# Expert rows added into one array of sums by accumulating scatters, and the last two experts' rows finished on their own

## The chip, the cores and the metric

The kernel runs on one core of a Trainium2 chip. The metric is the device time of one execution in microseconds; the profiled span runs from the first to the last instruction of one execution. Every data transfer runs on the core's 16 DMA engines, whichever queue issues it.

## The reference, cut to what matters

One encoder layer is computed for two inputs with the same parameters: 256 tokens of a prompt and 1024 of a sample, each of width D = 1024, in float32. After a mixer and a residual (`x1` below) comes a mixture of experts, and then the final norm:

```python
e = group * 8 + top2                      # two experts of one group for each token
y[t] = sum over its two experts of w * down(silu(x @ gate) * (x @ up))
out = rmsnorm(x1 + y, final_norm_g)
```

There are 32 experts in 4 groups of 8; a token picks one group and two experts inside it. The 1280 tokens of both inputs give 2560 expert rows of 1024 floats (4 KB each), and every token needs both of its rows before it can be normalised.

## The kernel before, in words

The kernel is written engine by engine, with semaphores set by hand. T = 1280 tokens are NT = 10 tiles of P = 128. The stages are: projection, mixer, output projection with the router (tile by tile), the experts, and a tail.

**The experts.** Step i treats expert i of an order that takes the four groups in turn (`expert_at`), so four experts in a row share no token. n_half is read at run time; here it is 16, so there are 32 steps (steps 0 to 3 are written out, the others stand in a loop of two steps per turn). A list in DRAM holds, for every expert, the rows of its tokens; positions beyond the list's length hold an index out of bounds, which an indirect transfer leaves out. In each step

- SP loads 12 pieces of 512 KB of weights (`piece_in`, L680) into a ring of NST = 12 slots `e_st`. A piece is loaded when the slot's last user is split.
- ACT rounds a piece to `e_hi` (`hi_part`, L1533) and DVE subtracts to get `e_lo` (`lo_part`, L2037), in rings of NRG = 6. PE multiplies (`product3`, L937 to L939): 8 gate and up pieces of expert i, then 4 down pieces of expert i-1.
- POOL gathers the token rows of a later expert (`rows_in`, L850), their weights (`weights_in`, L871), and scatters the output rows of expert i-2 (`rows_out`, L858 to L861) from `yo` to `y_dram` ("expert_rows"), once ACT and DVE have copied them from PSUM (`y_half`, L1600 and L2119). There are two buffers `yo`, and each `y_half` waits for the scatter before it on the same buffer.

`y_dram` has 2T rows: a token's first expert writes row t, its second row T + t. Which of the two is first is decided in the routing (`route_rest`, L2000 to L2005, with `swapped`, `entry` and `turn_sizes`), such that the first rows are all written early.

**The tail.** All of `x1` stays in SBUF. After the loop POOL adds the first rows of tiles 0 to 4 onto `x1` by five direct accumulating transfers (`add_rows`, L877), SP loads those of tiles 5 to 9 to free slots of `e_st` (L736), and, once the scatters of the last two experts have landed, SP loads the second rows of all ten tiles (L743). DVE adds (L2188, L2195), or PE does by products with the identity (`first_row_part` L1291, `second_row_part` L1299); ACT takes the sum of squares and the root (L1656, L1657), DVE scales (`final_norm`, L2199 and L2203), SP stores (L746).

The wait that separates the early part of the tail from its late part is SP's:

```python
            for b in range(2):
                sp.wait_ge(y_out[b], 16 * n_half)
            for t in LATE_ORDER:
                slot = late_slot(t)
                if slot < NT - N_ADDED:
                    sp.wait_ge(f_sum, slot + 1)
                sp.dma_start(spare(slot), y_dram[T + t * P:T + (t + 1) * P, :]).then_inc(e_load[slot], 16)
```

Each queue works in program order. POOL's DMAs, direct and indirect, share one queue of descriptors, SP's another.

Of the kernel before, what the change touches and what calls it, by code (L numbers as in the profile page):

```python
# [15 lines left out]
P = 128  # L16
# [5 lines left out]
def build(nc, x_prompt, x_sample, norm1_g, w_in, pool_w, pool_scale, gate_b, head_norm_g, w_out,  # L22
# [27 lines left out]
    y_dram = nc.dram_tensor("expert_rows", (2 * T, D), F32).ap()  # L50
# [49 lines left out]
    entry = const("entry", [P, NT, 2], I32)  # L100
    swapped = const("swapped", [P, NT])
    turn_sizes = const("turn_sizes", [P, 2])
# [119 lines left out]
    rows_to = mbuf("rows_to", [P, NT * E + 1], I32)  # L222
    row_of = mbuf("row_of", [P, 2], I32)
    row_to = mbuf("row_to", [P, 2], I32)
# [3 lines left out]
    w_row = at("w_row", ROWS + KB, [P, 2], F32)  # L228

    gf_b = at("gf_b", ROWS + 4 * KB, [P, D], F32)  # L230
    N_ADDED = 5

    def spare(slot):

        return e_st[:, slot, :, :].rearrange("p a n -> p (a n)")

    def early_slot(t):

        return t - N_ADDED

    def late_slot(t):

        return (5 + t) % NST

    LAST_ROUTED, LAST_OUT = 2, 0
    SQUARES = 3
    ON_PE = (2, 4, 5, 7, 8, 9)
    LATE_ORDER = (0, 2, 1, 3, 4, 5, 6, 7, 8, 9)
# [10 lines left out]
    with ctx:  # L259
# [3 lines left out]
        def sem(name):  # L263
# [28 lines left out]
        rows_added = [sem(f"rows_added{i}") for i in range(NT // 2)]  # L292
# [21 lines left out]
        gx_load = [sem(f"gx_load{i}") for i in range(2)]  # L314
        ehi_done, elo_done, piece_used, no_row, gx_zero, ext_ready, exhi_done, exlo_done = (
# [7 lines left out]
        f_out, f_sum, f_pe_sum, f_root, f_done = (  # L323
            sem(n) for n in ("f_out", "f_sum", "f_pe_sum", "f_root", "f_done"))
# [153 lines left out]

        def late_loads(t, last):

            return 16 * (last + (3 if late_slot(t) < NT - N_ADDED else 2))

        def sums_taken(t):

            return NT - N_ADDED + sum(x not in ON_PE for x in range(t + 1))

        def pe_sum(t):

            return two((0, 2, 6, 4)[ON_PE.index(t) % 4])

# [22 lines left out]
        def _(sp):  # L513
# [230 lines left out]
            for t in range(NT):  # L744
                sp.wait_ge(f_done, t + 1)
                sp.dma_start(tokens(t, y_prompt, y_sample), x1[:, t, :]).then_inc(f_out, 16)  # L746
            sp.wait_ge(f_out, 16 * NT)


        @block.gpsimd  # L750
        def _(pool):
# [46 lines left out]
            for part, size in enumerate((float(T), -float(T))):  # L798
                pool.memset(turn_sizes[:, part:part + 1], size).then_inc(pool_step, 1)
            pool.wait_ge(pool_step, 21)  # L800
# [18 lines left out]
            def entries_out(i):  # L819
                pool.wait_ge(slots_done, 2 * i + 2)  # L820
                for k in range(2):
                    pool.indirect_dma_start(
                        out=list_dram, out_offset=bass.IndirectOffsetOnAxis(ap=slot_i[:, i, k:k + 1], axis=0),
                        in_=entry[:, order[i], k:k + 1], in_offset=None).then_inc(list_out[i % 2], 16)

            for i, t in enumerate(order):
                pool.wait_ge(xn2_done, i + 1)
# [26 lines left out]

            def rows_out(i, b):
                pool.wait_ge(y_left, i + 1)
                pool.wait_ge(y_right, i + 1)
                pool.tensor_copy(row_to[:, b:b + 1], rows_to[:, bass.ds(i, 1)]).then_inc(row_placed, 1)  # L858
                pool.wait_ge(row_placed, i + 1)
                pool.sem_inc(pool_past, 1)  # L860
                pool.indirect_dma_start(  # L861
                    out=y_dram, out_offset=bass.IndirectOffsetOnAxis(ap=row_to[:, b:b + 1], axis=0),
                    in_=yo[:, b, :], in_offset=None, bounds_check=2 * T - 1, oob_is_err=False).then_inc(y_out[b], 16)

            def weights_in(i, b):

                if isinstance(i, int):
                    rows = rows_to[:, i:i + 1] if i else first_row[:, :]
                else:
                    rows = row_of[:, b:b + 1]  # L870
# [4 lines left out]

            def add_rows(t):
                pool.dma_start(x1[:, t, :], y_dram[t * P:(t + 1) * P, :], accum_op=ALU.add).then_inc(rows_added[t], 16)  # L877
# [16 lines left out]
            rows_in(3, 1)  # L894
            rows_out(0, 0)
# [13 lines left out]
            for b in range(2):  # L909
                pool.wait_ge(y_out[b], 16 * n_half - 32)  # L910
                pool.sem_inc(pool_past, 1)
            for t in range(N_ADDED):
                add_rows(t)
            for b in range(2):
                pool.wait_ge(y_out[b], 16 * n_half - 16)
                pool.sem_inc(pool_past, 1)
            for b in range(2):
                pool.tensor_copy(row_to[:, b:b + 1],
# [1320 lines left out]
```

## Time and profile before

| | |
|---|---|
| median of 3 runs | 1171.67 us (1170.9 to 1173.81) |
| profiled execution, its own time | 1169.87 us |
| its span | 1168.1 us |
| busy share of PE, DVE, ACT, POOL | 98%, 73%, 60%, 23% |
| DMA moved | 324.11 MB, mean 277 GB/s |
| packets of the two queues in use, share of 16 engines | SP 65.1%, POOL 10.5% |

A busy share is an average over all stages. The time of the profiled execution is 1.8 us above its span (start and end of the program lie outside), and 1.8 us below the median of the runs. Of the DMA queues, "hardware_dynamic" (q1) is SP's here and "software_dynamic" (q0) is POOL's; a share of 100% means that 16 engines were occupied all the time.

### The profile page before, as it was taken

What the parts mean: (1) busy time and instruction counts of PE and PEld (TensorE: products, weight loads), DVE (VectorE), ACT (ScalarE), POOL (GpSimd) and SP (SyncE); (2) the same over time, 40 slices, a digit from 0 to 9 for tenths busy, and PEclk for the clock granted to TensorE, in tenths of its full rate; (3) what the DMA queues carried; (4) which work ended last, traced back from release to release, by engine and by line L of the source; (5) the groups of instructions that cost most, each with busy time, mean ns of one, the idle gap of its engine ahead of it and who ended that gap; (6) DMA issues with size and microseconds to landing.
All of it is one profiled execution on the core that took longest, in us unless ns stands there. A gap on an engine that the chain in (4) does not pass through costs nothing.

```text
span 1168.1 us, 18708 instructions
## 1 busy us (share of the span) xinstructions
PE 1142.5 (98%) x5934; PEld 962.9 (82%) x5934; DVE 857.4 (73%) x1340; ACT 699.1 (60%) x1134; POOL 273.3 (23%) x348
## 2 busy tenths in 40 slices
PE   8999999999999999999999999999999999999987
PEld 8988888888889888887888888888888888888863
DVE  6649510134437766677899999999999999999957
ACT  6342241233438744334788787787887887887834
POOL 2200210001200012223142332332332325443320
PEclk9999999999999999999999999999999999999999
DMA  7312240446969644444999999999999999999989
GB/s 223 90 36 83 90 136 1 128 144 220 312 242 365 219 139 157 155 176 157 390 407 388 396 386 401 381 399 386 388 385 393 387 386 392 379 398 388 381 253 359
DMA packets 137795, 324.11 MB, mean 277 GB/s; under 512 B 25526, under 2 KB 62304, under 8 KB 137744
## 3 DMA queue, kind: packets, MB, share of 16 engines
q1 hardware_dynamic: 120032, 279.18, 65.1%
q0 software_dynamic: 17712, 44.27, 10.5%
q8 instruction: 30, 0.49, 0.2%
q14 instruction: 21, 0.17, 0.0%
HBM read 285.37 MB, written 51.12 MB: 288 GB/s over the span
## 4 chain that ended last, share of the span: by engine, by line
PE 63%; DMA 25%; DVE 6%; issue 3%; ACT 2%; SPq 0%; ACTq 0%; DVEq 0%; POOLq 0%
DMA e_st<-in_expert_w_down_dram 19%; PE psum L937 17%; PE psum L939 17%; PE psum L938 17%; DVE e_lo L2037 3%; DMA units<-mlstm_units 1%; PE psum L1127 1%; ACT e_hi L1533 1%; DMA e_st<-in_expert_w_gate_dram 1%; PE psum L1221 1%; PE psum L951 1%; PE psum L1062 1%; DMA e_st<-in_expert_w_up_dram 1%; PE psum L1063 1%; PE psum L1299 1%
## 5 line engine op out<-in xcount | busy, mean ns | idle before, releaser
L2037 DVE TENSOR_TENSOR e_lo<-e_st,e_hi 128x1024 fp32r<-128x1024 f32 x384 | 447.0, 1217 | 26.4 <-ACT e_hi L1533 25.6
L1533 ACT ACTIVATE e_hi<-e_st 128x1024 fp32r<-128x1024 f32 x384 | 388.3, 1056 | 50.8 <-DMA e_st<-in_expert_w_down_dram 35.1
L939 PE MATMUL psum<-e_hi,ex_lo 128*128 128x512 f32 x512 | 199.5, 390 | 0.0
L937 PE MATMUL psum<-e_hi,ex_hi 128*128 128x512 f32 x512 | 199.4, 389 | 0.0
L938 PE MATMUL psum<-e_lo,ex_hi 128*128 128x512 f32 x512 | 199.2, 389 | 0.0
L937 PE MATMUL psum<-xT_hi,w_hi 128*128 128x512 f32 (+1 forms) x432 | 151.1, 350 | 2.2 <-DVE w_lo L1673 1.4
L939 PE MATMUL psum<-xT_hi,w_lo 128*128 128x512 f32 (+1 forms) x432 | 149.4, 346 | 0.0
L938 PE MATMUL psum<-xT_lo,w_hi 128*128 128x512 f32 (+1 forms) x432 | 149.2, 345 | 0.0
L858 POOL COPY row_to<-rows_to 128x1 int32 (+1 forms) x30 | 46.6, 1554 | 295.2 <-DVE yo L2119 295.2
L937 PEld LDWEIGHTS psum<-e_hi,ex_hi 128*128 128x128 f32 x512 | 96.1, 188 | 20.2 <-DVE ex_lo L2108 0.2
L939 PEld LDWEIGHTS psum<-e_hi,ex_lo 128*128 128x128 f32 x512 | 96.1, 188 | 20.0
L938 PEld LDWEIGHTS psum<-e_lo,ex_hi 128*128 128x128 f32 x512 | 96.1, 188 | 19.9
L937 PE MATMUL psum<-e_hi,ht_hi 128*128 128x512 f32 x256 | 105.8, 413 | 3.5 <-DVE e_lo L2037 2.4
L939 PE MATMUL psum<-e_hi,ht_lo 128*128 128x512 f32 x256 | 100.9, 394 | 0.0
L938 PE MATMUL psum<-e_lo,ht_hi 128*128 128x512 f32 x256 | 100.6, 393 | 0.0
L937 PEld LDWEIGHTS psum<-xT_hi,w_hi 128*128 128x128 f32 x432 | 82.3, 191 | 12.3 <-DVE w_lo L1673 1.6
L1673 DVE TENSOR_TENSOR w_lo<-w_st,w_hi 128x1024 fp32r<-128x1024 f32 x21 | 25.6, 1222 | 90.0 <-ACT w_hi L1329 90.0
L939 PEld LDWEIGHTS psum<-xT_hi,w_lo 128*128 128x128 f32 x432 | 82.1, 190 | 9.9
L938 PEld LDWEIGHTS psum<-xT_lo,w_hi 128*128 128x128 f32 x432 | 82.3, 191 | 9.7
L937 PE MATMUL psum<-wo_hi,mix_hi 128*128 128x512 f32 x160 | 64.5, 403 | 0.0
L939 PE MATMUL psum<-wo_hi,mix_lo 128*128 128x512 f32 x160 | 62.6, 391 | 0.0
L938 PE MATMUL psum<-wo_lo,mix_hi 128*128 128x512 f32 x160 | 62.3, 389 | 0.0
(292 smaller groups left out, 1857.2 us busy)
## 6 DMA issues: line engine op xcount, KB each, us to landing
e_st<-in_expert_w_gate_dram SPq DMA_DIRECT2D x128, 512.0 KB, 13.6
e_st<-in_expert_w_up_dram SPq DMA_DIRECT2D x128, 512.0 KB, 13.7
e_st<-in_expert_w_down_dram SPq DMA_DIRECT2D x128, 512.0 KB, 14.5
mlstm_units<-stage SPq DMA_DIRECT2D x18, 640.0 KB, 3.9
w_st<-in_w_in_dram SPq DMA_DIRECT2D x20, 512.0 KB, 4.4
xn_scratch<-xn POOLq DMA_DIRECT2D x20, 512.0 KB, 3.9
stage<-gate_rows SPq DMA_DIRECT2D x18, 512.0 KB, 5.8
e_st<-expert_rows SPq DMA_DIRECT2D x15, 512.0 KB, 10.0
```

Source lines behind the costliest of these rows:

```text
L858: pool.tensor_copy(row_to[:, b:b + 1], rows_to[:, bass.ds(i, 1)]).then_inc(row_placed, 1)
L937: pe.matmul(out, a_hi, b_hi, start=start, stop=False)
L938: pe.matmul(out, a_hi, b_lo, start=False, stop=False)
L939: return pe.matmul(out, a_lo, b_hi, start=False, stop=stop)
L951: last = pe.transpose(psum[:, 4 + 2 * (t % 2) + k // 4, (k % 4) * P:(k % 4 + 1) * P], xn[:, t % 2, k:D:KD], ident[:, :])
L1062: pe.matmul(out, unit_part(n, H + h), state[:, d, h, :], start=True, stop=False)
L1063: last = pe.matmul(out, unit_part(n, h), v[:, ck, h, :], start=from_zero(step), stop=True)
L1127: last = pe.matmul(psum[:, 7, 0:NL], x1T[:, k, :], rw[:, k, :], start=(k == 0), stop=(k == KD - 1))
L1221: last = pe.transpose(psum[:, 2 + half, (k % 4) * P:(k % 4 + 1) * P], gx[:, b, k:D:KD], ident[:, :])
L1533: act.activation(e_hi[:, r, :, :], e_st[:, slot, :, :], ACT.Copy).then_inc(ehi_done, 1)
L1673: dve.tensor_tensor(w_lo[:, m % 4, :, :], w_st[:, m % 2, :, :], w_hi[:, m % 4, :, :].bitcast(F32), ALU.subtract).then_inc(wlo_done, 1)
L2037: dve.tensor_tensor(e_lo[:, r, :, :], e_st[:, slot, :, :], e_hi[:, r, :, :].bitcast(F32), ALU.subtract).then_inc(elo_done, 1)
```

## The change

One array `sum_dram` ("row_sums") of T rows takes the place of `y_dram` with 2T.

- In the output-projection stage POOL stores each tile of `x1` to `sum_dram`, ahead of the two stores of `xn2`.
- `rows_out` scatters with an addition (`compute_op=ALU.add`) at the token's row. The indices `tokens_to` are made from the lists by two POOL operations before the first scatter.
- The decision on which expert comes first (`swapped`, `entry`, `turn_sizes`) is gone, with two DVE operations per tile and three after the last tile.
- In the tail, SP waits until all scatters but those of the last two experts have landed and loads all ten tiles of sums over `x1`. Tiles are normalised and stored as they come. POOL gathers the sums of the last two experts' tokens to `gx`; DVE adds the rows from PSUM (`late_total`), and the finished rows go by four indirect scatters to the two outputs, after every tile's store has landed, since the tiles have stale values in those rows.
- The last expert's products go to other PSUM banks (`bank=0`), so PE doesn't wait for `y_half`; PE takes no part in the tail's sums. The filler products `keep_busy` alternate between two banks.

```diff
@@ SP, tail
             sp.wait_ge(elo_done, down_piece(last, 3)[0] + 1)
             for b in range(2):
-                sp.wait_ge(y_out[b], 16 * n_half - 32)
-            for t in range(N_ADDED, NT):
-                slot = early_slot(t)
-                sp.dma_start(spare(slot), y_dram[t * P:(t + 1) * P, :]).then_inc(e_load[slot], 16)
-            for b in range(2):
-                sp.wait_ge(y_out[b], 16 * n_half)
-            for t in LATE_ORDER:
-                slot = late_slot(t)
-                if slot < NT - N_ADDED:
-                    sp.wait_ge(f_sum, slot + 1)
-                sp.dma_start(spare(slot), y_dram[T + t * P:T + (t + 1) * P, :]).then_inc(e_load[slot], 16)
-            for t in range(NT):
-                sp.wait_ge(f_done, t + 1)
-                sp.dma_start(tokens(t, y_prompt, y_sample), x1[:, t, :]).then_inc(f_out, 16)
+                sp.wait_ge(y_out[b], 16 * n_half - 16)
+            for t in (0, 1, 2, 3, 8, 9, 4, 5, 6, 7):
+                sp.dma_start(x1[:, t, :], sum_dram[t * P:(t + 1) * P, :]).then_inc(e_load[t] if t < 8 else sum_load[t - 8], 16)
+            for t in TAIL:
+                if t in range(NT):
+                    sp.wait_ge(f_done, TAIL_AT[t] + 1)
+                    sp.dma_start(tokens(t, y_prompt, y_sample), x1[:, t, :]).then_inc(f_out, 16)
             sp.wait_ge(f_out, 16 * NT)
+            sp.wait_ge(late_out, 16 * 4)
@@ POOL
             for i, t in enumerate(order):
+                pool.wait_ge(x1_done, i + 1 if i < NT - 1 else NT + 1)
+                pool.dma_start(sum_dram[t * P:(t + 1) * P, :], x1[:, t, :]).then_inc(sums_out, 16)
                 pool.wait_ge(xn2_done, i + 1)
...
             def rows_out(i, b):
                 pool.wait_ge(y_left, i + 1)
                 pool.wait_ge(y_right, i + 1)
-                pool.tensor_copy(row_to[:, b:b + 1], rows_to[:, bass.ds(i, 1)]).then_inc(row_placed, 1)
-                pool.wait_ge(row_placed, i + 1)
-                pool.sem_inc(pool_past, 1)
+                token_rows(i, b)
                 pool.indirect_dma_start(
-                    out=y_dram, out_offset=bass.IndirectOffsetOnAxis(ap=row_to[:, b:b + 1], axis=0),
-                    in_=yo[:, b, :], in_offset=None, bounds_check=2 * T - 1, oob_is_err=False).then_inc(y_out[b], 16)
+                    out=sum_dram, out_offset=bass.IndirectOffsetOnAxis(ap=token_of[:, b:b + 1], axis=0),
+                    in_=yo[:, b, :], in_offset=None, bounds_check=T - 1, oob_is_err=False,
+                    compute_op=ALU.add).then_inc(y_out[b], 16)
...
-            for t in range(N_ADDED):
-                add_rows(t)
...
+            pool.wait_ge(ext_ready, 4 * n_half + 2)
+            pool.sem_inc(pool_past, 1)
             for b in range(2):
                 pool.indirect_dma_start(
-                    out=y_dram, out_offset=bass.IndirectOffsetOnAxis(ap=row_to[:, b:b + 1], axis=0),
-                    in_=yo[:, b, :], in_offset=None, bounds_check=2 * T - 1, oob_is_err=False).then_inc(y_out[b], 16)
+                    out=gx[:, b, :], out_offset=None, in_=sum_dram,
+                    in_offset=bass.IndirectOffsetOnAxis(ap=token_of[:, b:b + 1], axis=0),
+                    bounds_check=T - 1, oob_is_err=False).then_inc(late_load[b], 16)
...
+            pool.wait_ge(f_out, 16 * NT)
+            for b in range(2):
+                pool.wait_ge(f_done, TAIL_AT[f"late {b}"] + 1)
+                pool.indirect_dma_start(
+                    out=y_sample[0, :, :], out_offset=bass.IndirectOffsetOnAxis(ap=late_to[:, b:b + 1], axis=0),
+                    in_=yo[:, b, :], in_offset=None, bounds_check=S1 - 1, oob_is_err=False).then_inc(late_out, 16)
+                pool.indirect_dma_start(
+                    out=y_prompt[0, :, :], out_offset=bass.IndirectOffsetOnAxis(ap=token_of[:, b:b + 1], axis=0),
+                    in_=yo[:, b, :], in_offset=None, bounds_check=S0 - 1, oob_is_err=False).then_inc(late_out, 16)
@@ ACT, tail (root(x) waits for the tile's load, or for late_sum, then squares and root as before)
-            y_half(last_i - 1, 0, down_piece(last_i, 3)[0] + 1)
-            for c in range(1, 4):
-                hi_part(last_piece(last_i, c))
-            y_half(last_i, 1, last_piece(last_i, 3)[0] + 1)
+            hi_part(last_piece(last_i, 1))
+            hi_part(last_piece(last_i, 2))
             act.activation(wts[:, 3, 0:1], epsc[:, :], ACT.Sqrt)
+            hi_part(last_piece(last_i, 3))
+            for x in TAIL:
+                root(x)
@@ DVE, tail (TAIL = [0, 1, 2, 3, "late 0", 8, 9, 4, "late 1", 5, 6, 7])
+            lo_part(last_piece(last_i, 1))
+            lo_part(last_piece(last_i, 2))
+            final_norm(0)
+            lo_part(last_piece(last_i, 3))
+            for x in TAIL[1:]:
+                if x == 2:
+                    late_total(0)
+                if x == 9:
+                    late_total(1)
+                final_norm(x)
```

On POOL, the end of the program before, from the loop's last scatter on (`expert_rows` is `y_dram`; L877 are the direct accumulating transfers, L927 the scatters of the last two experts):

```order
L861 DMA expert_rows<-yo,row_to 2560x1024
L871 DMA w_row<-entry_weights,row_of 128x1
L902 ISA
L902 COMPARE_AND_BRANCH
L910 ISA
L877 DMA x_136<-expert_rows 128x1024 x5
L915 REGISTER_ALU
L918 ISA
L918 COPY row_to<-rows_to 128x1
L918 ISA
L918 COPY row_to<-rows_to 128x1
L927 DMA expert_rows<-yo,row_to 2560x1024 x2
```

and the same place now, behind the loop (`row_sums` is `sum_dram`; L893 gathers sums, L905 and L908 write to the outputs):

```order
L886 COPY token_of<-tokens_to 128x1
L886 ISA
L886 COPY token_of<-tokens_to 128x1
L890 ISA
L893 DMA gx<-row_sums,token_of 128x1024 x2
L897 TENSOR_SCALAR late_far<-token_of 128x2
L898 TENSOR_SCALAR late_to<-token_of 128x2
L900 TENSOR_TENSOR late_to<-late_to,late_far 128x2
L905 DMA out_dram<-yo,late_to 1024x1024
L908 DMA out_dram<-yo,token_of 256x1024
L905 DMA out_dram<-yo,late_to 1024x1024
L908 DMA out_dram<-yo,token_of 256x1024
```

The direct additions are gone (the scatters in the loop add), and four scatters to the outputs close the queue, the first of them behind the wait for all stores.

On DVE, the tail before, from the last weight piece's split (L2037) on:

```order
L2037 TENSOR_TENSOR e_lo<-e_st,e_hi 128x1024
L465 ISA
L2119 COPY yo<-psum 128x512
L2187 ISA
L2188 TENSOR_TENSOR x_136<-x_136,e_st 128x1024 x5
L2195 TENSOR_TENSOR x_136<-x_136,e_st 128x1024 x2
L2199 RECIPROCAL wts<-wts 128x1
L2203 SCALAR_TENSOR_TENSOR x_136<-x_136,wts,gf_b 128x1024
```

and now, from the split of the last piece but one (L1982 is `lo_part`, L2125 `late_total`, L2136 and L2139 `final_norm`):

```order
L1982 TENSOR_TENSOR e_lo<-e_st,e_hi 128x1024
L2136 RECIPROCAL wts<-wts 128x1
L2139 SCALAR_TENSOR_TENSOR x_133<-x_133,wts,gf_b 128x1024
L1981 REGISTER_ALU
L1982 TENSOR_TENSOR e_lo<-e_st,e_hi 128x1024
L2136 RECIPROCAL wts<-wts 128x1
L2139 SCALAR_TENSOR_TENSOR x_133<-x_133,wts,gf_b 128x1024
L2123 REGISTER_ALU
L2125 TENSOR_TENSOR yo<-gx,psum 128x1024
```

The split of the last weight piece stands behind the first tile's scaling, and nine additions have become two.

## Rows read from the trace of the kernel before

**Rows 1.** Windows: us, each engine's busy time, TensorE's clock, DMA share, GB/s.
```profile
600.00:700.00 100.00, 100.00 (x471) 83.67 (x470) 94.91 (x96) 81.48 (x98) 31.91 (x30) 1.00 1.01 392
1000.00:1100.00 100.00, 99.60 (x472) 82.87 (x471) 93.75 (x96) 81.79 (x96) 38.50 (x28) 1.00 1.01 388
```

**Rows 2.** Timeline of ACT: the gate's activation in two steps running.
```profile
595.49 0.60 ACT L1605 ACTIVATE sg<-psum 128x512 f32<-128x512 f32 x1 [1.61 <-PE psum L939]
613.26 0.60 ACT L1605 ACTIVATE sg<-psum 128x512 f32<-128x512 f32 x1 [1.61 <-PE psum L939]
```

**Rows 3.** ACT's wait and the weight loads' landings (L680), 600 to 700 us.
```profile
ACT e_hi L1533 <- DMA e_st<-in_expert_w_down_dram: 0.2, 1, 0.2
DMA to landing us min/median/max: 10.9/13.0/14.1
```

**Rows 4.** The same (us in total, times, longest), 1000 to 1100 us.
```profile
ACT e_hi L1533 <- DMA e_st<-in_expert_w_down_dram: 10.0, 17, 1.5
DMA to landing us min/median/max: 11.5/14.7/16.4
```

**Rows 5.** DMA queues, 600 to 1100 us: packets, MB, share of 16 engines.
```profile
q1 hardware_dynamic: 48480, 176.54, 91.5%
q0 software_dynamic: 9075, 18.42, 9.6%
```

**Rows 6.** DMA queues, 1117 to 1124 us, with the direct accumulating transfers.
```profile
q0 software_dynamic: 256, 0.93, 66.9%
q1 hardware_dynamic: 255, 0.95, 36.7%
```

**Rows 7.** DMA queues, 806 to 809 us, around one plain scatter of the loop.
```profile
q1 hardware_dynamic: 266, 0.98, 80.6%
q0 software_dynamic: 156, 0.24, 21.5%
```

**Rows 8.** Window 1131 to 1138 us (columns as in rows 1), and its DMA queues.
```profile
1131.00:1138.00 7.00, 7.00 (x27) 5.07 (x27) 3.68 (x3) 0.49 (x2) 1.00 (x1) 0.98 0.50 198
...
q1 hardware_dynamic: 209, 0.74, 26.1%
q0 software_dynamic: 232, 0.63, 23.4%
```

**Rows 9.** The chain that ended last: start us, us, what.
```profile
1104.26 20.32 DMA e_st<-in_expert_w_down_dram
...
1130.99 7.20 DMA expert_rows<-yo,row_to
```

**Rows 10.** Timeline of ACT in the tail: one tile's square and root.
```profile
1149.69 1.06 ACT L1656 ACTIVATE e_st<-x 128x1024 f32<-128x1024 f32 x1
...
1150.87 0.29 ACT L1657 ACTIVATE wts<-wts,epsc 128x1 f32<-128x1 f32 x1
```

**Rows 11.** DVE in the tail: two tiles' scalings, and the group of late additions.
```profile
1149.00 0.15 DVE L2199 RECIPROCAL wts<-wts 128x1 f32<-128x1 f32 x1
...
1150.39 0.16 DVE L2199 RECIPROCAL wts<-wts 128x1 f32<-128x1 f32 x1
...
L2195 DVE TENSOR_TENSOR x<-x,e_st 128x1024 f32<-128x1024 f32 x4 | 4.9, 1222 | 3.1 <-DMA e_st<-expert_rows 3.1
```

**Rows 12.** The stores of the outputs (L746): issue to landing.
```profile
DMA to landing us min/median/max: 2.9/5.0/7.8
```

**Rows 13.** The list scatters of 4-byte rows (L822): landing, and two issues running.
```profile
DMA to landing us min/median/max: 2.3/3.4/8.8
...
430.33 1.04 POOL L822 DMA_INDIRECT row_lists<-entry,slot_i  x1 [0.30 <-issue]
431.68 1.01 POOL L822 DMA_INDIRECT row_lists<-entry,slot_i  x1 [0.30 <-issue]
```

**Rows 14.** Window 1128 to 1131 us: TensorE's clock after a wait for weights.
```profile
1128.00:1131.00 3.00, 3.00 (x9) 2.32 (x8) 0.69 (x1) 1.60 (x2) 0.01 (x1) 0.50 1.01 326
```

**Rows 15.** Timeline of DVE in the last tile's routing: an operation that goes.
```profile
542.18 0.22 DVE L2003 SCALAR_TENSOR_TENSOR entry<-turn_sizes,swapped,rowval 128x2 int32<-128x2 f32 x1
```

More of the change, by code:

```diff
@@ L314, in build @@
         gx_load = [sem(f"gx_load{i}") for i in range(2)]
+        late_load = [sem(f"late_load{i}") for i in range(2)]
+        sum_load = [sem(f"sum_load{i}") for i in range(2)]
+        sums_out, late_sum, late_out = sem("sums_out"), sem("late_sum"), sem("late_out")
         ehi_done, elo_done, piece_used, no_row, gx_zero, ext_ready, exhi_done, exlo_done = (
@@ L477, in expert_at @@
             return (i % GR) * EPG + (i // GR) % EPG
[L479 to L489, printed above, removed]
         def load_half_steps(eng):
@@ L1206, in _ @@
             for t in range(NT):
-                last = pe.matmul(psum[:, 5, 0:E], onesb[:, :], chosen[:, t, :], start=(t == 0), stop=(t == NT - 1))
+                last = pe.matmul(psum[:, 6, 0:E], onesb[:, :], chosen[:, t, :], start=(t == 0), stop=(t == NT - 1))
             last.then_inc(totals_ready, 1)
@@ L1235, in gate_up, with down @@
                     last.then_inc(piece_used, 1)
-            def down(piece, i, b, turned=None):
+            def down(piece, i, b, turned=None, bank=4):
                 pe.wait_ge(htlo_done, i + 1)
-                wait(pe, y_left, i)
-                wait(pe, y_right, i)
+                if bank == 4:
+                    wait(pe, y_left, i)
+                    wait(pe, y_right, i)
                 for c in range(4):
@@ L1245, in down @@
                     for half in range(2):
-                        last = product3(psum[:, 4 + half, :], (ht_hi[:, b, c, :], ht_lo[:, b, c, :]),
+                        last = product3(psum[:, bank + half, :], (ht_hi[:, b, c, :], ht_lo[:, b, c, :]),
                                         (e_hi[:, r, half, :], e_lo[:, r, half, :]), c == 0, c == 3)
@@ L1275, in _ @@
             last_i = 2 * n_half - 1
[L1276 to L1312 removed]
+            down(lambda c: last_piece(last_i, c), last_i, 1, bank=0)
         @block.scalar
@@ L2201, in final_norm @@
+            def final_norm(x):
+                dve.wait_ge(f_root, TAIL_AT[x] + 1)
+                if x in range(NT):
+                    rms, out = wts[:, 3, x:x + 1], x1[:, x, :]
+                else:
+                    k = int(x == "late 1")
+                    rms, out = stat[:, 1, k:k + 1], yo[:, k, :]
+                link(dve.reciprocal(rms, rms))
+                if x == TAIL[0]:
                     dve.wait_ge(norms_in, 48)
-                out = x1[:, t, :].rearrange("p (a n) -> p a n", a=2)
@@ L2203, in final_norm @@
-                dve.scalar_tensor_tensor(out=out, in0=pe_sum(t) if t in ON_PE else out, scalar=wts[:, 3, t:t + 1],
-                                         in1=gf_b[:, :].rearrange("p (a n) -> p a n", a=2),
+                dve.scalar_tensor_tensor(out=out, in0=out, scalar=rms, in1=gf_b[:, :],
                                          op0=ALU.mult, op1=ALU.mult).then_inc(f_done, 1)
-            for t in range(N_ADDED, NT):
-                early_sum(t)
-            for t in range(NT + 2):
-                if t < NT and t not in ON_PE:
-                    late_sum(t)
-                if t >= 2:
-                    final_norm(t - 2)
+            lo_part(last_piece(last_i, 1))
```

163 lines of the change are left out of this document (52 added, 111 removed).

## The prediction

> **What bounds the kernel now.** I read the windows first, then the waits and landings of the weight loads, then the DMA queues, and the chain last. In the expert stretch PE is busy without a gap, DVE 94 to 95% and the DMA engines 101% (packets overlap a little), at some 390 GB/s [rows 1]. The step repeats every 17.77 us (613.26 - 595.49), with ACT waiting for PE before the activation [rows 2]: PE sets the pace there. But the DMA engines are no looser. Between 600 and 700 us ACT waits 0.2 us for weights, and a weight load lands 13.0 us after its issue [rows 3]; between 1000 and 1100 us it waits 10.0 us, and the landing takes 14.7 us [rows 4]. Weights thus come later from step to step while PE holds its pace: the DMA engines need slightly more than 17.77 us a step, and by 1000 us the cushion is used up. Work added to them has nowhere to hide. In the tail the chain goes through the last weight load (20.32 us in place of 14.7), the last expert's scatter, 7.20 us [rows 9], the second rows' loads, and DVE's scaling.
>
> **What a plain row and an added row cost an engine.** From 600 to 1100 us SP's queue moves 176.54 MB, 43,100 packets of 4 KB, in 91.5% of 16 x 500 us: 0.17 us each. POOL's moves 18.42 MB, 4,497 rows, over 28 gathers and 28 scatters: 80 rows each [rows 5]. Beside the direct accumulating transfers POOL's queue moves 0.93 MB, 227 rows, in 66.9% of 16 x 7 us: 0.33 us each, while a weight packet beside them keeps 0.18 (0.95 MB in 36.7%) [rows 6]. An addition costs an engine 0.33 - 0.17 = **0.16 us a row** more. These additions go from DRAM to SBUF; none from SBUF to DRAM is in the trace. I take the same price: it is one read of the source and one of the destination through the engine either way. Its bounds are 0 (the second read runs beside the first) and 0.33 (each read waits for the other and the write). [...]
>
> **Which engines pay.** Spread over all 16, 80 rows are 5 to an engine. The trace speaks against that. Where both queues are busy an engine takes a packet of each in turn, so that an even scatter would hold half of all engine time; around a scatter of 59 rows (0.24 MB) POOL's queue holds 21.5% of three microseconds [rows 7], as if it ran on some eight engines for 2.6 us. At 1131 to 1138 us, with the last scatters and some leftover loads, the engines are busy 0.50 of the time, although both queues have work left: about half of the engines work, the others are through [rows 8]. So eight engines carry most of each scatter, 8 to 10 rows, and they are the ones that come late. I take **8 rows on the busiest engine** (the list fills positions from 0, and the last 16 of 80 fall to others). Bounds: 5 and 10.
>
> **The loop.** Thirty scatters become additions (experts 0 to 29): 30 x 8 x 0.16 = **+38.4 us** on the engines that hold up the weights, bounds 0 to 30 x 10 x 0.33 = 99. A step becomes 17.8 + 1.3 = 19.1 us. POOL's own share is nothing: it waits for `yo` in every step, the copy of the indices replaces a copy, and the two operations on 320 indices stand in an idle stretch before the first scatter.
>
> **Before the loop.** Ten stores of x1 (512 KB each) go out in a stage in which the engines are half idle; the last is issued shortly before the stores of xn2 that the first gather waits for, which may cost up to its 8 x 0.16 = 1.3 us. Two DVE operations fewer in the last tile's routing (0.22 us the longer one [rows 15]) and three in the weights give back up to five times that. I take -0.3 in all, from bounds of +1.3 and -1.1.
>
> **The tail, rebuilt.** (1) The last weights were issued at 1104.3 and took 20.32 us because five additions (640 rows of 0.33) and five early loads ran beside them [rows 9]; now only the two gathers of late sums do, 2 x 8 rows x 0.16 = 2.6 us. They land at 1104.3 + 14.7 [rows 4] + 38.4 + 2.6 = 1160.0. (2) The gain vector and the first tile of sums follow in the same queue, 8 packets of 0.16 us an engine each: 1162.6. The waits before those loads (the split of the last step's down pieces, the scatters of experts 28 and 29) are over some 5 us earlier. (3) ACT's square and root, 1.06 to 1151.16 - 1149.69 = 1.5 us [rows 10], for the first tile: 1164.1. (4) DVE then has twelve scalings at 1.39 us (1150.39 - 1149.00), two late totals and the last split at 1.22 [rows 11]: 20.3 us, the last at 1184.4. ACT needs 12 x 1.5 = 18 and the loads and stores 20 x 1.3 = 26 us from 1160.0 on, so DMA keeps up with DVE to within a store or two: the last store lands 3 to 4 us later [rows 12], **1188**. (5) New: POOL then issues four scatters. It starts 0.9 us after its release, the next three follow at 1.35 us (431.68 - 430.33), and the last lands between 2.3 us (4-byte rows [rows 13]) and 7.2 us (behind other work [rows 9]) after its issue. Its rows are 4 KB, with the engines idle: 4 us. 1188 + 0.9 + 4.0 + 4.0 = 1196.9; with -0.3, **1196.6**, against 1168.1: **+28.5 us**.
>
> Without the loop's 38.4 the change would save 9.9 us, for it takes PE's sums and the wait for the last scatter off the end, and puts one round of stores and scatters on it. The sum is against the profiled execution of 1169.87, hence 1198.4; the median lies 1.8 above that execution: **1200 us**.
>
> A rule that speaks for a milder end: around a full stretch the rows show 388 to 392 GB/s [rows 1]. The Trainium skill, "DMA: Bandwidth & Descriptors", Where 436 GB/s comes from, puts the limit for transfers with HBM at about 358 GB/s on the HBM side. By that rule bytes count, not the busiest engine: 0.33 MB more to read a step. The measured rate is above it, so it isn't the limit here; its form of the sum is the first rival.
>
> **The rivals.**
> - *Even load.* If all 16 engines share the added work, or if total bytes decide: 30 x 80 x 0.16 / 16 = 24 us instead of 38.4, so about **1186**. For it: the engines are 101% busy on average. Against it: rows 7 and 8. Chance 0.15.
> - *The second read is free* (faster, the other side). If an addition from SBUF reads its two sources, in two memories, side by side, a row costs 0.17 us as before, the step stays at 17.8, and the tail's 9.9 us are all that is left: **1162**. It decides below 9.9 / 240 = 0.04 us more a row. Against it: 0.33 in rows 6, where the sources also lie in two memories. Chance 0.11.
> - *Dearer additions*, another 0.17 us a row: 240 x 0.17 = 41 us more, **1241**. Chance 0.06.
> - *TensorE's clock.* After waiting for the last weights PE ran at 0.50 of its clock, 1.2 GHz [rows 14]. If the 1.3 us that PE now waits in each step bring that about now and then, steps grow further; at 3 us of half clock a step (1.5 us lost, of which 1.3 were idle anyway) and some restarts, +10: **1210**. Chance 0.06.
> - *Nothing measurable:* the cushions before and in the loop take all and the tail is as long as before, **1171**. A measurement can tell about 0.3% from no change. Chance 0.02.
>
> **How the numbers follow.** My forecast keeps 0.60. The range of 1182 to 1217 takes in the even load and the clock, and 9 or 10 rows on the busiest engine (+5 to +10), and leaves out the free read, the dearer one and no change, 0.19. Faster 0.11, same 0.02, slower 0.87.
>
> **What would show it.** The gate's activations 19.1 us apart late in the loop; POOL's scatter packets at 0.33 us (q0 near 13% of the engines with some 80 rows a transfer); ACT's waits for weights 1 to 2 us a step from the start, and PE waiting for `e_lo`; landings of weight loads near 15.5 us; a last weight landing near 1160; DVE without gaps for 20 us; some 9 us from the last store to the end. Wrong if activations stay 17.8 us apart (the read is free), or are 18.6 apart (even load), or if PE's clock leaves 1.00 in the loop.

## The result, and the profile after

| | before | after |
|---|---|---|
| median (range, runs) | 1172.74 us (1170.9 to 1179.68, 4) | 1198.75 us (1196.06 to 1201.53, 4) |
| profiled span | 1168.1 us | 1195.9 us |
| first and last activation of the gate | 563.8, 1112.1 | 564.7, 1150.2 |
| from the last activation to the end | 56.1 us | 45.7 us |

After against before is 1.0228, with an interval of 1.02 to 1.0257: slower. 1200 us was predicted.

The gate's activation runs once in a step, 32 times. Its group shows first and last start in one row, and so where a difference lies. Below is the group in the trace after (min/median/max in ns, first and last start in us).

```profile
L1551 ACT ACTIVATE sg<-psum x32: 574/581/602, 564.7 to 1150.2; 128x512 f32<-128x512 f32 x32
```

In the trace before it is this row:

```profile
L1605 ACT ACTIVATE sg<-psum x32: 577/597/602, 563.8 to 1112.1; 128x512 f32<-128x512 f32 x32
```

From the first to the last it was 548.2 us and is 585.5 (the timelines have 563.84 to 1112.05 and 564.66 to 1150.19): the 31 steps between them take 37.3 us more, and what follows takes 10.3 less (the start of the experts is 0.8 later). The net is the 27.8 us between the spans. The first of the 31 steps takes some 14 us in both traces; the 30 behind it take 17.8 us each before and 19.0 now.

The windows of the loop in the trace after, columns as in [rows 1]:

```profile
600.00:700.00 100.00, 97.28 (x456) 80.37 (x455) 92.20 (x95) 79.43 (x92) 28.27 (x26) 1.00 1.01 372
1000.00:1100.00 100.00, 95.51 (x446) 78.20 (x445) 88.53 (x89) 78.97 (x90) 27.00 (x25) 1.00 1.01 369
```

PE no longer fills the window, while the DMA engines stay at 101% with fewer bytes: 372 and 369 GB/s in place of 392 and 388 [rows 1]. The same occupation moves less. The DMA queues from 600 to 1100 us show whose packets grew:

```profile
q1 hardware_dynamic: 45359, 165.16, 86.4%
q0 software_dynamic: 8464, 17.50, 13.9%
```

POOL's queue holds 13.9% with 17.50 MB, where it held 9.6% with 18.42 MB [rows 5]. That is 0.26 us for a 4 KB row in place of 0.17, over gathers and scatters together; the gathers are half of them, so a scattered row costs about 0.35. Two of the waits, ACT's for weights and PE's for `hh` from DVE, first from 600 to 700 us (us in total, times, longest):

```profile
ACT e_hi L1479 <- DMA e_st<-in_expert_w_down_dram: 7.4, 10, 2.4
...
PE psum L1237 <- DVE hh L2070: 2.5, 2, 1.5
```

And from 1000 to 1100 us; the last line is the landings of the weight loads (L655) in the same stretch:

```profile
ACT e_hi L1479 <- DMA e_st<-in_expert_w_down_dram: 12.5, 14, 2.7
...
PE psum L1237 <- DVE hh L2070: 4.5, 4, 1.6
...
DMA to landing us min/median/max: 12.2/16.2/17.1
```

From 600 to 700 us ACT already waits 7.4 us for down weights, where it waited 0.2 [rows 3], and from 1000 to 1100 us a load lands after 16.2 us in place of 14.7 [rows 4]. The cushion that lasted up to 1000 us before is gone by 600. What PE waits for is `hh`, which DVE makes behind the splits of the late weights, and hardly ever `e_lo`, which the forecast had named. The chain that ended last says the same from the other side:

```profile
DMA e_st<-in_expert_w_down_dram 30%; PE psum L918 13%; PE psum L920 13%; PE psum L919 13%; DVE e_lo L1982 5%; ACT e_hi L1479 2%; PE psum L1044 2%; PE psum L1108 1%; PE psum L1043 1%; PE psum L1051 1%; SPq L655 1%; PE psum L932 1%; DVE x L2139 1%; PE psum L1089 1%; PE psum L964 1%
```

Thirty per cent of the whole span are landings of down weights, where the chain of the kernel before had 19%. The tail's chain, start and length in us:

```profile
1165.92 1.28 DVE x L2139
...
1179.59 1.30 DVE x L2139
1180.90 2.64 DMA out_dram<-x
...
1184.44 0.38 POOL out_dram L905
...
1185.80 1.00 POOL out_dram L908
...
1188.38 0.97 POOL out_dram L908
```

DVE scales without a gap, the last store lands at 1183.54, and the four scatters are issued between 1184.4 and 1189.35. The span ends at 1195.9, 6.5 us after the last issue is done. In that stretch the trace has one instruction left on POOL's sequencer, DRAIN, at the end of its program. It starts at 1185.9, lasts 9.8 us and is over at 1195.7; the other engines end behind it.

```profile
L245 POOLq DRAIN  x1: 9825/9825/9825, 1185.9 to 1185.9; - x1
```

### The profile page after: what moved, and what is told of

It reads as the page before. It is cut to its first block, busy times and chain, and to the rows that moved or that the text cites. A ratio compares the mean times of both kernels' runs of the same rounds, so it can differ in the third digit from the quotient of the medians.

```text
span 1195.9 us, 18493 instructions
## 1 busy us (share of the span) xinstructions
PE 1124.7 (94%) x5846; PEld 949.8 (79%) x5846; DVE 852.1 (71%) x1311; ACT 709.6 (59%) x1138; POOL 280.0 (23%) x360
## 4 chain that ended last, share of the span: by engine, by line
PE 50%; DMA 33%; DVE 8%; issue 4%; ACT 3%; SPq 1%; POOL 0%; ACTq 0%; POOLq 0%; DVEq 0%
DMA e_st<-in_expert_w_down_dram 30%; PE psum L918 13%; PE psum L920 13%; PE psum L919 13%; DVE e_lo L1982 5%; ACT e_hi L1479 2%; PE psum L1044 2%; PE psum L1108 1%; PE psum L1043 1%; PE psum L1051 1%; SPq L655 1%; PE psum L932 1%; DVE x L2139 1%; PE psum L1089 1%; PE psum L964 1%
## 5 line engine op out<-in xcount | busy, mean ns | idle before, releaser
L1982 DVE TENSOR_TENSOR e_lo<-e_st,e_hi 128x1024 fp32r<-128x1024 f32 x384 | 451.8, 1222 | 61.2 <-ACT e_hi L1479 59.8
L1479 ACT ACTIVATE e_hi<-e_st 128x1024 fp32r<-128x1024 f32 x384 | 397.4, 1058 | 101.3 <-DMA e_st<-in_expert_w_down_dram 56.4
L826 POOL COPY token_of<-tokens_to 128x1 int32 (+1 forms) x30 | 39.1, 1303 | 333.8 <-DVE yo L2064 333.8
L918 PE MATMUL psum<-e_hi,ht_hi 128*128 128x512 f32 x256 | 108.6, 424 | 2.2 <-DVE e_lo L1982 2.2
```

The source lines that it names most:

```text
L826: pool.tensor_copy(token_of[:, b:b + 1], tokens_to[:, bass.ds(i, 1)]).then_inc(row_placed, 1)
L918: pe.matmul(out, a_hi, b_hi, start=start, stop=False)
L1479: act.activation(e_hi[:, r, :, :], e_st[:, slot, :, :], ACT.Copy).then_inc(ehi_done, 1)
L1982: dve.tensor_tensor(e_lo[:, r, :, :], e_st[:, slot, :, :], e_hi[:, r, :, :].bitcast(F32), ALU.subtract).then_inc(elo_done, 1)
```

## The experiments

The theory is the forecast's: an accumulated row holds an engine 0.16 us longer, eight rows of every scatter fall on the busiest engine, and its weights are late by that much. Rivals: the load is even over the engines or total bytes decide; the addition is slow as such, whatever the engine load (PE's clock, a mode of the queue); or the tail has a hidden loss. All ratios are to the kernel before, run beside them on the same chip.

**1. Plain scatters** in the place of the accumulating ones.

```diff
-                    compute_op=ALU.add).then_inc(y_out[b], 16)
+                    ).then_inc(y_out[b], 16)
```

> The changed kernel with the addition taken out of the loop's scatters (they overwrite; the expert rows are not summed). Everything else, the tail too, is as changed. My theory: an added row costs a DMA engine 0.33 us in place of 0.17, and nothing else in the change slows the loop. The gate's activations stand 17.8 us apart again, the scatters land in 7.5 us instead of 9.5, and the time falls by some 38 us to about 1161, some 10 us under the kernel before. Rival, the loop is slower through something else (the indices' copy, PSUM banks, the extra 5 MB of sums): the time stays near 1199. Rival, PE's clock: if the half-speed spells of the changed kernel were a cause and not an effect, they and part of the 38 us would stay.

Measured: 1164.78 us (1160.99 to 1166.62), ratio 0.9944 (0.9918 to 0.997). The activations run from 566.3 to 1114.4, 548.1 us, as before the change. The loop's loss is therefore the addition's alone. From the last activation to the end it is 48.6 us (1163.0 - 1114.4), 2.9 more than in the changed kernel, and all of that lies behind the last scatter's issue: 10.4 us to the end (1152.6 to 1163.0) in place of 7.5. Experiment 9 takes this up.

**2. The rows scattered twice, plainly.** The second copy goes to an array of its own, and the thresholds of the waits are doubled.

```diff
+                pool.indirect_dma_start(
+                    out=twin_dram, out_offset=bass.IndirectOffsetOnAxis(ap=token_of[:, b:b + 1], axis=0),
+                    in_=yo[:, b, :], in_offset=None, bounds_check=T - 1, oob_is_err=False).then_inc(y_out[b], 16)
```

> The changed kernel with every scatter of the loop done twice without an addition, once to a second array and once to the sums (expert rows are not summed). My theory: what counts is time on the busiest DMA engines, 8 rows of 0.16 us more a step, whether by an addition or by a second copy. Step 19.1 us, time 1199, as in the changed kernel, within 5 us. Rival, an addition is dearer through its read of the destination, or hinders the weight loads otherwise than by its engine time: then this one is faster than the changed kernel by more than 5 us. POOL has one more scatter of 1.35 us to issue, hidden by its waits of 11 us a step.

Measured: 1192.11 us (1190.41 to 1195.84), ratio 1.0177 (1.0151 to 1.0203). The last activation is at 1149.17 us. Its queues from 600 to 1100 us:

```profile
q1 hardware_dynamic: 45533, 165.79, 86.7%
q0 software_dynamic: 12436, 26.35, 13.5%
```

13.5% of the engines' time with half as many bytes again, 384 GB/s in all, and the loop is as slow as with additions. Occupation decides, not the addition as such. The ratio is 5 thousandths (6 us) under that of the changed kernel, a little over the 5 us that the expectation had set as the sign of a dearer addition; the intervals just overlap (1.02 and 1.0203). But 3.5 us of it lie behind the last scatter's issue, 4.0 us to the end here (1190.1 to 1194.1) against 7.5. The loop takes 581.5 us, like experiment 10's 581.0, so no run shows an addition dearer than a second copy.

**3. The changed kernel with its lists spread over all engines.** An expert's list fills the positions 0, 64, 4, 68 and so on in place of 0, 1, 2.

```diff
+                link(dve.tensor_scalar(slot_k[:, 1, :], slot_k[:, 0, :], 0x20, 6, ALU.bitwise_and, ALU.logical_shift_left))
+                link(dve.tensor_scalar(slot_k[:, 2, :], slot_k[:, 0, :], 0x3C0, 1, ALU.bitwise_and, ALU.logical_shift_left))
+                link(dve.tensor_scalar(slot_k[:, 3, :], slot_k[:, 0, :], 0xC00, 5, ALU.bitwise_and, ALU.logical_shift_right))
...
-            pool.iota(slot_ramp_i[:, 0:P], pattern=[[E, P]], base=0, channel_multiplier=0).then_inc(pool_step, 1)
+            pool.iota(slot_ramp_i[:, 0:P].rearrange("p (h s c) -> p h s c", h=2, s=16),
+                      pattern=[[E, 2], [2 * E, 16], [32 * E, 4]], base=0, channel_multiplier=0).then_inc(pool_step, 1)
```

> The changed kernel, correct sums, with the positions of each expert's list permuted so that 80 rows fall on all 16 DMA engines, 5 to each, in place of 8 on the first eight (seven small DVE operations more per tile of the routing). My theory, the busiest engine decides: per step 96 weight packets, 5 gathered rows and 5 added rows (10 packets' time) are 111 packets' time, against 120 in the changed kernel and 112 in the kernel before. The step goes back to PE's 17.8 us and the time to about 1161. Rival, the engines' total decides (even load): the total is unchanged, so the step stays at 18.9 us and the time at 1196 to 1199.

Measured: 1160.01 us (1159.11 to 1161.94), ratio 0.9913 (0.989 to 0.9937). The activation, and then the queues from 600 to 1100 us:

```profile
L1553 ACT ACTIVATE sg<-psum x32: 597/597/598, 564.8 to 1110.9; 128x512 f32<-128x512 f32 x32
```

```profile
q1 hardware_dynamic: 48715, 177.39, 88.7%
q0 software_dynamic: 9104, 18.48, 14.3%
```

POOL's queue holds 14.3% with 18.48 MB, 0.25 us a row and so 0.34 for a scattered one: the additions cost the engines what they cost in the changed kernel, and the loop takes 546.1 us. The whole loss is gone with the same additions, the same bytes and the same issues; only the position of a row in its list, and with it the engine, differs. This is the run that decides. No view names the engine of a packet, so the run shows that the positions matter and the engine stays the reading of them; a port or another thing tied to the position was not tested apart from it. The rival of the even load falls with it: if total engine time or bytes decided, this kernel would be as slow as the changed one.

**4. The kernel before with its lists spread.** The same edit, on the kernel before.

> The kernel before with the same permutation of the lists. My theory: the busiest engines go from 112 to 106 packets' time a step; PE sets the pace already, so little is won: the weight loads land in 10 us or less instead of 14, ACT's waits for weights in the loop vanish, and the time falls by 1 to 4 us, to about 1169. Rival, total load decides: no change in landings or time.

Measured: 1166.43 us (1164.9 to 1169.6), ratio 0.9962 (0.9941 to 0.9983). The activations run from 565.84 to 1113.66, 547.8 us, so the loop gained nothing measurable (the tail is 4.4 us shorter); a weight load lands in 6.7 us (median, 600 to 1100 us) in place of 14.1. In the kernel before, the landings grew late but PE was hardly held up. The uneven lists cost little there; they took the cushion that the additions needed. With spread lists on both sides the change is a gain: 0.9913 in experiment 3 against 0.9962 here, with intervals that don't touch, so one array of sums is about 0.5% faster once the rows are spread.

**5. Additions in every second step only.**

```diff
-                    compute_op=ALU.add).then_inc(y_out[b], 16)
+                    **({"compute_op": ALU.add} if b else {})).then_inc(y_out[b], 16)
```

> The changed kernel, but only the scatters of the odd steps (buffer 1) are accumulating ones, 15 of the 30; those of the even steps write plainly (the rows of the experts of the even steps are not summed). Busiest-engine theory with both limits reached at once (the DMA engines stand at PE's pace before the change): the loss in the loop is half, 15 x 8 x 0.16 = +19 us, steps of 18.4 on the average, ratio near 1.009. If there were still a cushion, a threshold below which additions are free, half the additions would cost clearly less than half: +5 us or less in the loop, ratio near 0.997. If the loss came once and for all from accumulating at all (PE's clock falling, a mode of the queue), it would be near the whole 37 us, ratio 1.02.

Measured: 1177.62 us (1176.24 to 1183.23), ratio 1.0058 (1.0036 to 1.0079).

```profile
L1551 ACT ACTIVATE sg<-psum x32: 577/590/602, 567.0 to 1128.7; 128x512 f32<-128x512 f32 x32
```

561.7 us from first to last is 13.5 more than before, against 37.3 with all additions. The cost grows with their number, so nothing is lost once and for all; half of them cost 36% (by the ratios, from experiment 1 as the zero, 40%). On the busiest engine the 15 additions weigh 15 x 8 x 0.16 = 19.2 us, of which 13.5 are lost; the 30 weigh 38.4, of which 37.3, 32.8 (experiment 10) and 31.4 (experiment 8, whose loop is the changed kernel's) are lost, 33.8 in the mean. Both leave some 5 us, as if they found a cushion where I had set none. That isn't shown: loops paced by transfers differ by 6 us between profiles (experiment 10), and by the ratios half of the additions cost 0.0114 where half of the whole loss is 0.0142, a difference as large as the intervals leave open.

**6. Spread lists, and the scatters to the prompt output ahead of the last stores.** A semaphore of their own (`f_prompt`) for the stores of the two prompt tiles lets these two scatters go early.

```diff
-            pool.wait_ge(f_out, 16 * NT)
+            pool.wait_ge(f_prompt, 32)
             for b in range(2):
                 pool.wait_ge(f_done, TAIL_AT[f"late {b}"] + 1)
...
+            pool.wait_ge(f_out, 16 * (NT - 2))
+            for b in range(2):
```

> The changed kernel with the lists spread over all 16 engines (as in the run before with that edit) and the two scatters of the last experts' rows to the prompt output issued as soon as the two prompt tiles are stored, so that only the two to the sample output stand behind the last store. Issues of these scatters follow each other by 1.35 us: the end comes 2.7 us earlier than with the spread alone, about 1157.5 us, ratio 0.989 to the kernel before. If the end is set by something else behind the last landing, the time stays at 1160, ratio 0.991.

Measured: 1161.26 us (1156.59 to 1164.49), ratio 0.989 (0.9865 to 0.9915). Against experiment 3's 0.9913 the gain would be the 2.7 us expected, but the intervals overlap: not resolved. In the traces the stretch from the issue of the last store to the end is 13.7 us in place of 15.8. The loop is experiment 3's and takes 547.3 us, though its loads land in 14.0 us (median, 600 to 1100 us) where experiment 3 has 11.9. Both versions beat the kernel before and the changed one.

**7. Spread lists with plain scatters** (experiments 1 and 3 together).

> The changed kernel with spread lists and with plain scatters in place of the accumulating ones (expert rows not summed). With five rows to an engine in place of eight the engines have a cushion of about 3 x 2 x 0.17 = 1 us a step, as much as the 30 x 5 x 0.16 = 24 us of additions need in the whole loop (0.8 us a step). Busiest-engine theory: the additions hide, the steps stay at 17.75 us and the time is within 2 us of the spread kernel with additions (ratio to the kernel before 0.990 to 0.992). Total-work theory (each addition delays weights by its share of all engine time however spread): 10 us or more faster than the spread kernel with additions, ratio 0.983 or less.

Measured: 1161.21 us (1160.14 to 1164.02), ratio 0.9903 (0.9883 to 0.9923). First the activation, then the queues from 600 to 1100 us with the loads of down weights (count, KB, median us from issue to landing):

```profile
L1552 ACT ACTIVATE sg<-psum x32: 597/597/601, 566.0 to 1111.9; 128x512 f32<-128x512 f32 x32
```

```profile
q1 hardware_dynamic: 49009, 178.46, 91.7%
q0 software_dynamic: 9105, 18.47, 9.6%
...
e_st<-in_expert_w_down_dram SPq DMA_DIRECT2D x113, 512.0 KB, 8.1
```

545.9 us for the loop, against 546.1 with additions. Where each engine has five rows, an addition costs nothing measurable in the loop. It shows in the landings alone: 8.1 us here, 12.5 in experiment 3. The total times hide a difference at the end: 10.4 us from the last issue to the end here, 7.1 in experiment 3.

**8. The changed kernel without its last four scatters.** The wait for these scatters goes too.

```diff
-            pool.wait_ge(f_out, 16 * NT)
-            for b in range(2):
-                pool.wait_ge(f_done, TAIL_AT[f"late {b}"] + 1)
...
@@ SP
-            sp.wait_ge(late_out, 16 * 4)
```

> The changed kernel without the four scatters of the last two experts' rows behind the last store and without the wait for them (the rows of the last two experts are left out of the outputs). In the trace of the changed kernel the last store lands at 1183.5 us and the last scatter at about 1191, with 5 us to the end of the span. The round costs 0.9 + 3 x 1.35 + 2.6 = 7.5 us: ratio 1.0165 to the kernel before. If stores and scatters share a fixed end (a final barrier that already overlaps the scatters), less than 4 us, ratio 1.020.

Measured: 1183.39 us (1181.75 to 1191.33), ratio 1.0113 (1.0078 to 1.0149): 13 us, where both theories gave less. In its trace the tail is 9.3 us shorter than in the trace after (36.4 against 45.7), and the loop came out 6 us shorter too, though it is the same. Two runs took the two apart.

**9. The same on the spread lists**, where PE and not the weights set the loop's pace.

> The kernel with spread lists, without the four scatters of the last two experts' rows and without the wait for them (those rows are left out of the outputs). Here the loop runs at PE's pace, so that only the tail differs from the kernel with spread lists. In the run of the changed kernel without these scatters the ratio fell by 0.0115 (13 us), where its profiled tail is 9.3 us shorter; if the round alone is 7.5 to 10 us, this run comes out at 0.983 to 0.985 of the kernel before; if it is really 13 us, at 0.980.

Measured: 1149.16 us (1147.62 to 1151.22), ratio 0.9803 (0.9768 to 0.9837), 0.0110 or 12.9 us below experiment 3. The loops are alike here (546.3 and 546.1 us), so the round costs 11 to 13 us, more than I had given it in either place. In this trace the last store is issued at 1142.3 and the span ends at 1147.0:

```profile
L715 SPq DMA_DIRECT2D out_dram<-x x10: 332/332/338, 1123.5 to 1142.3; - x10
```

With the scatters, in experiment 3, it is issued at 1141.6 and the span ends at 1157.4. POOL's issues behind it there:

```profile
L907 POOL DMA_INDIRECT out_dram<-yo,late_to x2: 970/1014/1057, 1146.3 to 1149.0; - x2
L910 POOL DMA_INDIRECT out_dram<-yo,token_of x2: 972/988/1004, 1147.7 to 1150.3; - x2
```

Start of the last issue to the end of the span: 7.1 us in experiment 3, 7.5 in the trace after (1188.4 to 1195.9) and in experiments 5 and 10, 7.7 in experiment 6, but 10.4 in experiments 1 and 7 and 4.0 in experiment 2. The landings of the changed kernel's last scatters (L908) took

```profile
DMA to landing us min/median/max: 2.6/2.6/2.7
```

so 4.8 us pass after the last one has landed (1188.4 + 2.7 = 1191.1). In experiment 9, with the same gathers and scatters in the loop but none near the end, 0.4 us pass after the last store's landing. The rest belongs to POOL's DRAIN: in all eight traces with scatters last the span ends 0.2 us after it. It lasts 9.8 us after, 9.4 in experiment 3, 12.7 in experiments 1 and 7 and 6.3 in experiment 2. The kernel before has it too, from 1130.8 to 1142.8 (first line), and in experiment 9 it starts at 1121.6 (second line):

```profile
L259 POOLq DRAIN  x1: 12056/12056/12056, 1130.8 to 1130.8; - x1
L246 POOLq DRAIN  x1: 9631/9631/9631, 1121.6 to 1121.6; - x1
```

There the tail hides it. What sets its length stays open: it is no matter of additions alone, since experiments 1 and 2 both have none, and their DRAINs last 12.7 and 6.3 us.

**10. The changed kernel once more, with no edit.**

> The changed kernel once more, with no edit, beside the others of this job. Theory that the loop of the changed kernel wanders from run to run because the weights set its pace (1143.8 and 1150.2 us for the last activation in two profiles with the same loop): ratio between 1.018 and 1.026, last activation between 1143 and 1152 us. If the last scatters are worth 13 us by themselves, it stays at 1.0228 and 1150 us.

Measured: 1196.72 us (1194.93 to 1201.92), ratio 1.0216 (1.0166 to 1.0265).

```profile
L1551 ACT ACTIVATE sg<-psum x32: 577/584/602, 565.6 to 1146.6; 128x512 f32<-128x512 f32 x32
```

581.0 us of loop, against 585.5 in the first trace and 579.6 in experiment 8. A loop paced by transfers varies by some 6 us between profiles, where all loops paced by PE lie within 2.3 us of each other (545.9 to 548.2). From the last activation to the end it is 48.6 us here, 45.7 in the first trace. Against this run experiment 8 is 1.4 us shorter in the loop and 12.2 in the tail (36.4 against 48.6), so its 13 us were the round's after all, as experiment 9's 12.9 are.

## Why the prediction was right, step by step

- **The sum.** A span of 1196.6 was forecast, 1195.9 came out; the median was 1198.75 instead of 1200. The mechanism is shown by experiments 1, 3 and 7 together: no loss without additions, none with additions on even lists. That the median was met within 1.3 us is partly luck: the profiles of one loop differ by 6 us, and experiment 10 comes to nearly the same span (1195.2) with 4.5 us less in the loop and 2.9 more in the tail.
- **Price of an added row, +0.16 us.** The queue rows give 0.35 us for an added row (0.34 in experiment 3) and 0.17 for a plain one: +0.17 to 0.18, a little above the forecast. The packets say the same one by one: of POOL's 4 KB packets from 600 to 1100 us, all but a few take about 0.16 us in the trace before, and in the trace after half take 0.16 and nearly all others 0.33. The bounds of 0 and 0.33 are excluded. The price of the accumulating transfers from DRAM held for those from SBUF.
- **Eight rows on the busiest engine.** Right: experiment 3 undoes it and the loss goes. The Trainium skill, "DMA: Bandwidth & Descriptors", The descriptor swizzle, assigns positions 0 to 63 of a 128-partition transfer to engines 0 to 7. By that rule a list of 80 that fills from 0 puts eight rows on each of these. The runs agree, since positions 64 and up in turn with them remove the loss; no view shows the engines themselves.
- **The loop, +38.4.** Measured +37.3, +32.8 and +31.4 in three profiles, 33.8 in the mean; the first one, which the result stands on, happens to be the nearest. Behind the first step the activations are 19.0, 18.9 and 18.9 us apart in the mean, near the 19.1 that was given as the sign and above the 18.6 of the even load. The term rests on both limits being reached from the first step on. The mean and experiment 5 speak for a cushion of some 5 us (the waits of [rows 3] are nearly nothing at 600 us), which the sum had named and not subtracted; within the scatter of the profiles it isn't shown.
- **Before the loop, -0.3.** +0.8 in the trace after, within the +1.3 that was given as a bound; the starts of the experiments scatter between 564.2 and 567.7, so this term is smaller than what one profile can tell.
- **The tail.** The total of -9.9 came out as -10.3 (-7.5 in experiment 10), by errors that cancel. The last weights were issued at 1142.4 as forecast (1142.7) but took 11.5 us and not 17.3: they landed at 1153.9, where I had 1160.0. That term was 5.8 us too large: it took the loop's landing and added the gathers' rows, and why the last load was faster than the loop's was not looked into. The first scaling follows ACT's root at 1160.9, 3.2 us early. DVE needed 20.0 us (20.3 forecast), and the last store landed at 1183.5 (1188 forecast). The round behind it took 12.4 us, where the sum had 8.9. The step that failed is (5): I counted issues and a landing (0.9 + 4.0 + 2.7 measured = 7.6) and set the end at the landing. The 4.8 us behind it are the rest of POOL's DRAIN. No row that I had read shows it, but the trace before has it, 12.1 us long and hidden by the tail (experiment 9).
- **The rivals.** The even load (1186) is excluded by experiment 3, the free read (1162) by the queue rows, dearer additions (1241) and no change (1171) by the time. Experiment 7 moves 394 GB/s from 600 to 1100 us on this core; the limit of about 358 GB/s that the Trainium skill gives ("DMA: Bandwidth & Descriptors", Where 436 GB/s comes from) is not one here. The Trainium skill, "Collectives: The Full Stack", The bandwidth ceiling, explains for ring collectives that a reducing step runs at about half the rate of a copy, because its two source reads go on the same ring. The scatters here have that ratio: 0.33 to 0.35 against 0.17 us.
- **TensorE's clock.** This forecast was wrong in the small: the clock did leave 1.00 in the loop, which was named as a sign of being wrong. Below is such a window, in the columns of [rows 1].

```profile
961.50:967.50 6.00, 5.19 (x14) 4.22 (x15) 5.95 (x8) 3.73 (x5) 0.00 (x0) 0.50 0.88 332
```

The granted clock is 0.50, the lower level of 1.2 GHz, while DVE is busy all the time. The trace after has four such stretches behind the start of the loop, 17.0 us together. Experiments 3 and 7, where PE never waits in the loop, have none there, but experiment 5, where PE waits 9.4 us, has none either: the low clock comes only in loops with waits, and not in all of them. What it costs in a loop that waits for weights anyway was not measured apart. Across the profiles it doesn't go with the loop's length: 6.8 us of low clock in experiment 2 (581.5 us), 13.6 in experiment 8 (579.6), 20.4 in experiment 10 (581.0), 17.0 in the trace after (585.5). So it is little, and the rival of 1210 is not borne out.

## What to carry to other kernels

An indirect transfer whose list fills positions from 0 and leaves out the rest loads the DMA engines unevenly; before adding engine time per row, count rows on the busiest engine and spread the positions over all. An accumulating scatter costs two rows of engine time, and it is free or fully paid according to whether that engine has slack against the engine that sets the pace: look for the slack in landings (from 600 to 1100 us 14.1 in the kernel before against 6.7 in experiment 4), not in the mean DMA share, which reads 101% in both cases. The landings are a guide and no threshold: with spread lists and additions they were 11.9 to 14.0 us in experiments 3, 9 and 6, and the loop lost nothing. And indirect transfers at the very end of a program cost more than their landing, because the program's end waits for POOL's DRAIN, 6 to 13 us long here. Issue POOL's last transfer early enough for its DRAIN to end under other work (it was over 12.7 us after POOL's last issue in experiment 9, 13.6 in experiment 8), and look for the DRAIN row in the trace. Moving all four scatters that far ahead was not tried.

## What the runs showed of the hardware that was not expected

- With indirect transfers last, the program ends with POOL's DRAIN, which lasted 6.3 to 12.7 us in eight traces. The end came 4.0 to 10.4 us after the last issue started, 4.8 us behind the landing in the changed kernel; where plain stores are last it came 0.4 us behind the landing (experiments 8 and 9).
- A DMA share of 101% doesn't tell how close the engines are to holding up the work. It stood there in the kernel before and in experiment 4 alike, while the landing of a weight load fell from 14.1 us to 6.7.
- Loops paced by transfers vary by 6 us between profiles of the same loop, loops paced by PE by about 2.
